# One decoder step on one core: sample rows in four copies, small matmuls in row and column strips, gathers in pairs

## The reference

```python
# HGRN2, 4 heads of 128; sample sequences bring a state of their own
S = exp(g_last)[..., None] * S + einsum('bshd,bshv->bhdv', k_dec, v)
# SSD (Mamba-2), 8 heads of 64, 2 groups of B and C
w = cb[..., None] * exp(rel) * dt[:, None]
y = einsum('btsgr,bsgrp->btgrp', w, x) + ...
h = exp(c_last)[..., None, None] * h + einsum('bsgrp,bsgn,bsgr->bgrpn', x, B, w_in)
# experts: two of eight for each token
top_v, top_i = top_k(logits, 2); top_w = softmax(top_v)
for e in range(8):
    out = out + combine[..., e:e + 1] * swiglu(h, w_up[e], w_down[e])
```

## Time and profile before

| | |
|---|---|
| median of 3 runs | 2414.25 us (2412.71 to 2416.66) |
| profiled execution | 2419.2 us |
| its span | 2417.0 us |
| TensorE busy | 2356.0 us (97%), 19532 instructions |
| VectorE, ScalarE, GpSimd busy | 582.5, 409.6 and 134.4 us |
| mean granted TensorE clock | 0.975 of full speed |
| DMA | 535.16 MB, mean 221 GB/s |

### The profile page before, as it was taken

One profiled execution on the slowest core, in us unless ns is written; L12 is line 12 of the kernel. 1 busy time (PEld: TensorE's weight loads), 2 busy tenths in 40 slices (PEclk: granted clock), 3 DMA queues, 4 the chain that ended last, 5 costly groups with the idle time before them and its releaser, 6 DMA issues.

```text
span 2417.0 us, 43667 instructions
## 1 busy us (share of the span) xinstructions
PE 2356.0 (97%) x19532; PEld 1507.8 (62%) x19532; DVE 582.5 (24%) x1124; ACT 409.6 (17%) x763; POOL 134.4 (6%) x137
## 2 busy tenths in 40 slices
PE   7999999989999999999999889999999999999999
PEld 6777667757777778776777653535353535353535
DVE  4383313423110027622244211010101010101010
ACT  3323313311000023323232010000000000000000
POOL 1121120000000002111100000000000000000000
PEclk9999989989999999999999889999999999999999
DMA  5335324574443543443355449999999999999993
GB/s 155 114 103 150 118 74 136 156 187 122 137 130 108 164 126 107 126 122 109 114 153 155 111 187 415 416 382 364 364 362 359 363 360 367 354 368 358 363 361 137
DMA packets 290393, 535.16 MB, mean 221 GB/s; under 512 B 10936, under 2 KB 222010, under 8 KB 273824
## 3 DMA queue, kind: packets, MB, share of 16 engines
q1 hardware_dynamic: 290208, 532.38, 62.8%
HBM read 518.50 MB, written 13.85 MB: 220 GB/s over the span
## 4 chain that ended last, share of the span: by engine, by line
PE 94%; DVE 2%; SPq 1%; DMA 1%; ACT 1%; issue 1%; DVEq 0%; ACTq 0%
PE bank L911 91%; PE bank L917 3%; DMA mem<-in_cache_kv_w_dram 1%; ACT mem L1731 1%; DVE mem L2423 0%; SPq L614 0%; DVE col L2426 0%; DVE mem L2134 0%; DVE mem L2439 0%; DVE mem L2436 0%; SPq L632 0%; DVE mem L2138 0%; DVE mem L2434 0%; SPq L616 0%; SPq L615 0%
## 5 line engine op out<-in xcount | busy, mean ns | idle before, releaser
L911 PE MATMUL bank<-mem 128*32 128x256 f32 (+9 forms) x14656 | 1404.0, 439 | 27.0 <-DMA mem<-in_cache_kv_w_dram 8.7
L911 PEld LDWEIGHTS bank<-mem 128*32 128x32 f32 (+3 forms) x14656 | 770.0, 124 | 628.5 <-issue 422.5
L911 PE MATMUL bank<-hflat,mem 128*128 128x288 f32 (+1 forms) x2944 | 736.3, 416 | 7.8 <-DMA hflat<-in_cache_kv_w_dram 7.8
L911 PEld LDWEIGHTS bank<-hflat,mem 128*128 128x128 f32 (+1 forms) x2944 | 549.8, 192 | 170.5 <-issue 19.9
L1731 ACT ACTIVATE mem<-bank 128x288 f32<-128x288 f32 (+9 forms) x443 | 198.1, 465 | 1273.4 <-PE bank L911 717.4
L2134 DVE TENSOR_TENSOR xT<-xT,bank 128x288 f32<-128x288 f32 x72 | 28.4, 450 | 496.2 <-PE bank L911 496.2
L1731 ACT ACTIVATE mem<-mem 128x1152 f32<-128x1152 f32 (+8 forms) x103 | 80.4, 780 | 133.7 <-DVE mem L2357 91.1
L2138 DVE SCALAR_TENSOR_TENSOR mem<-mem,bank 128x288 f32<-128x288 f32 (+1 forms) x93 | 43.2, 479 | 241.6 <-ACT mem L1731 204.2
L917 PE MATMUL bank<-ident,mem 128*128 128x128 f32 (+3 forms) x642 | 88.7, 272 | 10.3 <-DMA mem<-in_x_sample_dram 7.3
L917 PEld LDWEIGHTS bank<-ident,mem 128*128 128x128 f32 (+3 forms) x642 | 68.3, 142 | 37.9 <-issue 25.9
L2134 DVE TENSOR_TENSOR mem<-mem 128x1152 f32<-128x1152 f32 (+5 forms) x65 | 71.4, 1099 | 10.0 <-POOL mem L838 5.2
(11 more groups left out here) (200 smaller groups left out, 725.5 us busy)
## 6 DMA issues: line engine op xcount, KB each, us to landing
mem<-in_w_moe_up_dram SPq DMA_DIRECT2D x64, 2048.0 KB, 10.4
mem<-in_w_moe_down_dram SPq DMA_DIRECT2D x56, 2048.0 KB, 10.8
mem<-in_w_moe_up_dram SPq DMA_DIRECT2D x32, 2304.0 KB, 10.4
mem<-in_w_in_dram SPq DMA_DIRECT2D x70, 1024.0 KB, 5.2
mem<-in_w_moe_up_dram SPq DMA_DIRECT2D x16, 1536.0 KB, 8.7
mem<-in_w_ffn_up_dram SPq DMA_DIRECT2D x44, 512.0 KB, 5.1
mem<-in_cache_kv_w_dram SPq DMA_DIRECT2D x24, 512.0 KB, 6.0
mem<-in_w_ffn_down_dram SPq DMA_DIRECT2D x16, 704.0 KB, 4.7
```

Of the source, the lines that this page charges most:

```text
L911: return mm(out, lhsT, rhs, start=start, stop=stop, skip_group_check=True)
```

## The change

1. **Sample rows on all partitions.** `token_rows` makes block 2 by four matmuls with the identity, one in each column strip of 32, so that the 32 sample rows stand four times on the 128 partitions. (Not for the keys and values of attention.) The step sizes (`dt_rows`, table `tokc`) likewise. Copies that read them cover 128 partitions.
2. **State sums as two row strips.** A mask `halfm` (partitions x 4) takes the place of `seqm`: partitions 0 to 63 pick sequences 0 to 3, partitions 64 to 127 pick 4 to 7. `vexp` and `bexp` get half as long, and the two matmuls of a state sum contract over rows 0 to 63 and 64 to 127. GpSimd makes `halfm` at the start, by a memset and eight selections.
3. **SSD heads in pairs.** The broadcasts of heads h and h + 1 stand together behind every second tile, and `ssd_y` computes both heads of the pair before, two tiles after their broadcasts, with its matmuls alternating between the two column strips of 64. VectorE's, ScalarE's and GpSimd's programs follow.
4. **Gathering in pairs.** `Pm` and `hg` are doubled (the second `hg` in the space of the step sizes), a gather matmul streams the slots of two experts (192 columns), and TensorE gathers behind slab 15 (feature tiles 0 to 5, into banks 0 to 2) and slab 18 (tiles 6 and 7, into bank 0 again) of every second expert. ScalarE drains by eight copies of 192 columns.

```diff
-        vexp = view(arena, A1 + 4736, DB, P)
+        vexp = view(arena, A1 + 4736, DB // 2, P)
...
+            step(gp.memset(halfm[:, :], 0.0))
+            for first in (0, 80):
+                for i in range(DS):
+                    step(gp.affine_select(out=halfm[:, :], in_=halfm[:, :], compare_op=ALU.not_equal, fill=1.0,
+                                          base=-first - i, pattern=[[-DS, DB // 2]], channel_multiplier=1))
...
-            def token_rows(key, src, blk, tiles):
+            def token_rows(key, src, blk, tiles, fourfold=True):
                 t0, n = BLK[blk]
                 acc = open_bank(key)
                 for i, m in enumerate(tiles):
-                    ins = turn(acc[0:n, P * i:P * i + P], src[:, m, t0:t0 + n])
+                    if blk == 2 and fourfold:
+                        for r in range(0, P, TS):
+                            ins = put(acc[r:r + TS, P * i:P * i + P], src[:, m, TP:T], ident[:, :])
+                    else:
+                        ins = turn(acc[0:n, P * i:P * i + P], src[:, m, t0:t0 + n])
...
             def hgrn_state(L, h):
                 pe.wait_ge(*at("vexp_ready", L, h + 1))
                 for k in range(2):
-                    acc = open_bank(("hg_s", L, h, k))
-                    ins = put(acc[:, :], kdtok[0:TS, 2, P * h:P * h + P],
-                              vexp[0:TS, 4 * k:4 * k + 4, :].rearrange("p b v -> p (b v)"))
+                    acc, rows = open_bank(("hg_s", L, h, k)), slice(64 * k, 64 * k + 64)
+                    ins = put(acc[:, :], kdtok[rows, 2, P * h:P * h + P], vexp[rows].rearrange("p b v -> p (b v)"))
                     close_bank(ins, ("hg_s", L, h, k))
...
+                pe.wait_ge(*at("w_ready", L, 2 * j + 2))
+                parts = [(0, TP, P, 0, 0), (P, TP, P, 1, TP), (TP, T, TS, 2, 384)]
+                for i, (c0, c1, n, b, w0) in enumerate(parts):
+                    for e in range(2):
+                        c = P * j + 64 * e
+                        ins = put(acc[64 * e:64 * e + 64, c0:c1], xdt[0:n, b, c:c + 64],
+                                  wb[e][0:n, w0:w0 + c1 - c0], i == 0, i == 2)
+                    yield
...
                 h = t - AT_EVENT
-                if 0 <= h < SH:
+                if 0 < h <= SH and h % 2 == 0:
+                    yield from ssd_y(L, h // 2 - 1)
+                if 0 <= h < SH and h % 2 == 0:
                     yield from ssd_head(L, h)
+                    yield from ssd_head(L, h + 1)
...
+            def gather(it, banks, m0):
+
+                for i in range(2 * len(banks)):
+                    m = m0 + i
+                    acc = bank[banks[i // 2]][:, 2 * CAP * (i % 2):2 * CAP * (i % 2) + 2 * CAP]
+                    for b in range(3):
+                        ins = put(acc.rearrange("p (e c) -> p e c", e=2), htok[:, b, P * m:P * m + P],
+                                  Pm_pair[:, :, CAP * b:CAP * b + CAP], b == 0, b == 2)
+                    if i % 2:
+                        ins.then_inc(*lup("m_gathered"))
...
-                        if n == 15 and e < NEXP - 1:
-                            gather(it + 1)
+                        if n == 15 and e % 2 and e < NEXP - 1:
+                            gather_most(it + 1)
+                        if n == 18 and e % 2 and e < NEXP - 1:
+                            gather_rest(it + 1)
...
-                select(expert(r, 0), 0)
+                pick_pair(expert(r, 0), 0)
+                weights()
+                weigh_slots(expert(r, 0), 0)
...
                     gate("A")
+                    if e % 2 and e < NEXP - 1:
+                        pick_pair(it + 1, e + 1)
                     if e < NEXP - 1:
-                        select(it + 1, e + 1)
+                        weigh_slots(it + 1, e + 1)
```

More of the change, by code:

```diff
@@ L193, in hybrid_decoder @@
         hidT = view(arena, 0, 7, TT, P)
-        hg = view(arena, 2688, KT, CAP)
-        Pm = view(arena, 3456, 3, CAP)
+        PM_GAP = 10280 - 3456
+        Pm = [view(arena, 3456 + PM_GAP * i, 3, CAP) for i in range(2)]
+        Pm_pair = arena[:, 3456:3456 + 2 * PM_GAP].rearrange("p (e x) -> p e x", e=2)
         Pc = view(arena, 3744, 3, TT, P)
@@ L1099, in dt_rows @@
                         c = 24 * b + 8 * i
-                        ins = turn(acc[0:n, c:c + 8], dts[0:SH, r, t0:t0 + n])
+                        if b == 2:
+                            for at0 in range(0, P, TS):
+                                ins = put(acc[at0:at0 + TS, c:c + 8], dts[0:SH, r, TP:T], ident[0:SH, 0:SH])
+                        else:
+                            ins = turn(acc[0:n, c:c + 8], dts[0:SH, r, t0:t0 + n])
                         if b == 2 and i == 2:
@@ L1588, in _, with gather_most, gather_rest @@
             nr = load_rounds(pe)
[L1590 to L1600 removed]
+            def gather(it, banks, m0):
[7 more added lines that the diff above has]
+                        ins.then_inc(*lup("m_gathered"))
+            def gather_most(it):
+                pe.wait_ge(*lat("m_pick", it, 2))
+                pe.wait_ge(*lat("m_gated", it, 0))
+                gather(it, (0, 1, 2), 0)
+            def gather_rest(it):
+                pe.wait_ge(*lat("m_hg", it, 2))
+                gather(it, (0,), 6)
             scatter_bank = up_bank + y_bank[0:1]
@@ L1620, in _ @@
             with pe.Fori(0, nr) as r:
-                gather(expert(r, 0))
+                gather_most(expert(r, 0))
+                gather_rest(expert(r, 0))
                 for e in range(NEXP):
@@ L1634, in slab_product @@
                                 for q in range(4):
-                                    ins = put(bank[out[b]][32 * q:32 * q + 32, 0:f], hg[:, k, 32 * b:32 * b + 32],
+                                    ins = put(bank[out[b]][32 * q:32 * q + 32, 0:f], hg[e % 2][:, k, 32 * b:32 * b + 32],
                                               w[:, i, f * q:f * q + f], k == 0, k == KT - 1)
@@ L1915, in mixer @@
                         act.wait_ge(*at("hg_done", L))
-                    if 0 <= t - AT_EVENT < SH:
-                        ssd_decays(L, t - AT_EVENT)
+                    if 0 < t - AT_EVENT <= SH and (t - AT_EVENT) % 2:
+                        for e in range(2):
+                            ssd_decays(L, t - AT_EVENT - 1 + e)
                     if t < 2:
@@ L2071, in gathered_out @@
             def gathered_out(it):
-                for half in range(2):
-                    act.wait_ge(*lat("m_gathered", it, half + 1))
-                    fn(hg[:, 4 * half:4 * half + 4, :], bank[half][:, 0:4 * CAP].rearrange("p (a b) -> p a b", a=4),
-                       ACT.Copy).then_inc(*lup("m_hg"))
+                for i in range(4):
+                    act.wait_ge(*lat("m_gathered", it, i + 1))
+                    src = bank[i % 3][:, 0:4 * CAP].rearrange("p (m e c) -> p m e c", m=2, e=2)
+                    for x in range(2):
+                        fn(hg[x][:, 2 * i:2 * i + 2, :], src[:, :, x, :], ACT.Copy).then_inc(*lup("m_hg"))
             with act.Fori(0, nr) as r:
@@ L2328, in ssd_rows @@
                 dve.wait_ge(st_out, 16 * (2 * L + 1))
-                for b, (t0, n) in enumerate(BLK):
+                for b in range(3):
                     key = ("xtok", L, b)
@@ L2697, in _ @@
             dve.wait_ge(top_apart, 1)
-            step(ve.memset(Pm[:, 2, :], 0.0))
+            for i in range(2):
+                step(ve.memset(Pm[i][:, 2, :], 0.0))
             key = ("rank", 0)
```

130 lines of the change are left out of this document (57 added, 73 removed).

## The result

The changed kernel takes 2383.8 us (median of 4 runs, 2382.33 to 2388.57); the kernel before took 2415.45 on the same chip (2412.71 to 2420.34). The medians differ by 31.7 us; the ratio is 0.9865, 95% interval 0.9847 to 0.9884. The forecast was 2380, range 2368 to 2393. The profiled execution of after is the longest of the four: 2388.57 us with a span of 2386.9, against 2419.2 and 2417.0 before.

What follows compares the result with a forecast made beforehand. TensorE, busy 2356.0 of 2417.0 us, was taken as the bound. Terms 11.5 + 6.9 + 1.6 + 11.2 - 2.2 - 2.0 + 7 gave 34.0 us less, so a median of 2380, 8 in 10 range 2368 to 2393.

Steps and rivals of the forecast that it cites:

- expert pairs: Expert stage: gathering two experts over 192 columns gains 14.9 us at later pairs, loses 3.4 at the first: 11.5 gained.
- HGRN2 sums: Eight HGRN2 state sums: two row strips of 64 run at once, 0.86 us less each, 6.9 gained.
- SSD sums: Eight SSD state sums: same packing, but the second strip waits for VectorE to empty its bank; 1.6 us gained.
- heads and y: SSD heads: broadcasts and outputs in pairs, five visits a layer instead of nine; 11.2 us gained in two layers.
- fourfold rows and step sizes: Sample rows and step sizes made in four column strips: 1.0 plus 1.2 us, together 2.2 lost.
- start: Kernel start: GpSimd's extra mask delays the constants TensorE waits for; 2.0 us lost.
- clock in the mixers: Behind SSD state sums, 14 of 34 us at half clock vanish: 7 us gained; none expected behind HGRN2 heads.
- the clock stays as it is: Rival: four-column matmuls alone pull the clock down, so low clock remains: 2387 us, chance 0.14.
- Strips that don't overlap: Rival at the state sums: row strips of 64 run one after another; 8.5 us less gain, 2389, chance 0.07.
- slabs that set the pace: Rival in the expert stage: DMA sets the pace, TensorE's saving returns as waits; 14.9 less gain, 2395, chance 0.05.
- weights loaded in series: Rival at the expert gathers: each instruction waits for its own weight load; 2402 us, chance 0.02.
- a late pair: Rival at the SSD heads: y waits for its pair's weights and TensorE stands; some 2425 us, chance 0.04.

Runs made afterwards that it cites:

- first and last groups: Sets of kernels sharing a chip with the kernel before, at 2417.65 us (first) and 2413.8 us (last); the changed kernel, unedited, took 2382.1 and 2380.64 us there.
- experiment 2: Changed kernel with the gathering of one expert at a time put back: 2394.34 us.
- experiment 4: Changed kernel with both matmuls of each state sum on the same 64 partition rows (wrong state): 2394.39 us.
- experiment 3: Changed kernel with the SSD head outputs and decay broadcasts one head at a time again: 2392.61 us.
- experiment 6: Changed kernel with GpSimd making the two-half mask behind the constants instead of ahead of them: 2380.58 us.
- experiment 12: Kernel before the change with only the last two attention cache loads put ahead of the output weights: 2402.81 us.
- experiment 5: Changed kernel with both matmuls of each state sum over all 128 partition rows (wrong state): 2389.36 us.
- experiment 7: Changed kernel with seven of the eight four-column products of each SSD state group left out (wrong sample heads): 2364.19 us.
- experiment 8: Changed kernel with the last two attention cache loads issued ahead of the 1 MB output weights on the same queue: 2371.48 us.

## Why the prediction was right

The mechanism was right in the terms of packing and pairing; the added rows were priced too high, and the clock term came near its amount partly by luck. The forecast stood 34.2 under before's median; measured are 31.7, and 35.6 and 33.2 in the first and last groups. By its terms, the measured side from the table (mean of three executions after) and the experiments:

| term | forecast | measured | shown by |
|---|---|---|---|
| expert pairs | -11.5 | -11.0 | table; 10.8 in experiment 2 |
| HGRN2 sums | -6.9 | -6.4 | table at full clock; 6.8 in experiment 4 |
| SSD sums | -1.6 | -1.6 | 0.20 a sum in the rows; 1.8 in experiment 4 |
| heads and y | -11.2 | -11.8 | experiment 3 |
| fourfold rows and step sizes | +2.2 | about 0 | 15.7 to 15.8 busy; 0.99 to 1.01 from start to start |
| start | +2.0 | +2.3 | experiment 6 (2.7 over 12 executions, 2.9 in the table) |
| clock in the mixers | -7 | -6.3 | 51.2 us low before, 38.7 after in the mean; 3.4 of it behind the SSD sums |
| attention | 0 | -1.4 | table; +1.9, -3.3 and -2.8 in single executions |

The measured terms add up to 36.2 us less, or 35.6 with the table's 2.9 for the start; the three profiled spans are in the mean 35.6 shorter than before's (2381.5 against 2417.0).

**Experts.** The step held with its price. The first part of a later pair in after, grouped by shape (count, busy us, mean ns):

```profile
L921 PE MATMUL bank<-mem 128*128 128x192 f32 x36 | 6.1, 329 | 0.0
```

Without the last one's 0.33 that is 5.8 us for 35, 0.165 each where 0.163 was forecast. The first gather lost what was said: six selections take 2.13 in place of 1.05, and from its first matmul to the next slab product are 11.60 us in place of 9.45, together 3.2 against a forecast of 3.4.

**State sums, heads.** Right to a few tenths, including the half that the SSD sum can't win because VectorE holds the bank. The doubt about row strips of 64 is settled by experiment 4.

**The added rows.** This term was mis-sized. I took 15% more for four column strips from the scatter, where four strips of rows carry 288 columns each. Four column strips over 128 rows cost 0.02 us for a group of 32 instructions in place of 8, and no more for the step sizes (0.30 against 0.28).

**The clock.** The amount is near and the place is in good part wrong. The step that failed is "I take 14 of the 34 us as gone": behind the SSD sums 6.8 us of low clock went (34.1 to 27.3, or 10.2 from the 37.5 of experiment 12), which is worth 3.4 to 5.1 us and not 7. This part repeats, for 27.3 stands in all nine executions with two strips and all four-column products. The rest of the 6.3 lies behind the HGRN2 heads (17.1 before; 13.7, 10.2 and 10.2 after), from which I expected nothing. That it belongs to the change isn't shown: over the ten profiled executions whose HGRN2 part is the changed kernel's, the low clock there wanders between 6.8 and 20.5 us, 13.3 in the mean, against 17.1 in both with before's mixers. So the total was met partly by luck. At the SSD sums the sums' packing (experiments 4 and 5, and 12) and the four-column products (7) both have their part, and pairing the heads has none (3). That TensorE idles before a drop is not needed: it is busy for 10.00 of the 10 us ahead of each of the six drops behind the SSD sums in after. In the attention, less idling went with less low clock (experiment 8). The Trainium skill ("TensorE: Matmul & The Clock Gate", Part 1, HAM oscillation) lays such drops to idling: the trace agrees with it in the attention, and not behind the SSD sums.

**The rivals.** That the clock stays as it is would have been 2387, only 3 us from what was measured, so the time alone doesn't rule it out. The clock record does, by the 27.3 us behind the SSD sums in place of 34.1 and 37.5. Its reason, the four-column products, is right for about half of what is left (13.7 of 27.3 us in experiment 7). Strips that don't overlap, slabs that set the pace, weights loaded in series and a late pair each left the mark they were to leave nowhere.

## What to carry to other kernels

When TensorE is the bound, look for small matmuls by what they leave unused: products of few rows go side by side as row strips, 64-column products as column strips, and two products with the same weights become one; each gave what its instruction times said to within a tenth. Take the clock out before you judge a stretch, and profile the same kernel twice before you explain 3 us. And look at what stands ahead of a load in its queue: moving one line of issues gave a third of what the whole change gave.

## What was not expected of the hardware

- Four 32-column strips of 128-row matmuls cost the same as one: 116 instructions 15.7 us busy, 284 instructions 15.8; from start to start 8 take 0.99 us and 32 take 1.01.
- The height of a tile costs nothing here, another height next to it does: two matmuls over 512 columns take 1.72 us at 128 rows among 128-row tiles, 1.91 at 64 rows, and 1.06 as two strips.
- Low clock can fall behind a TensorE that never idles: 10.00 of 10 us busy ahead of each drop behind the SSD sums. And it shrinks with the waits: in experiment 8 each attention stretch idled about 5 us less and had 6.8 to 6.9 us less of low clock, though only 1.1 to 1.2 us of its busy time went.
- An issue can hold the issuing engine for microseconds: the first part of one cache load took 3.00 to 5.71 us to issue with weights ahead of it, 0.60 without.
